# Mask added by TensorE, convolution tiles per pair of channel blocks, and a recurrent unit without reciprocal, in a two-part transformer kernel

## The reference

```python
# recurrent unit of the even layer (width 512, both directions)
log_a = -LRU_C * gate_a * softplus(-lam)
a = exp(log_a)
mult = sqrt(-expm1(2.0 * log_a))
u = mult * gate_x * xc
# h_f, h_b: scans of h = a * h + u forwards and backwards; the result is h_f + h_b

# neighbourhood attention of the odd layer (16 heads of 64, 4 rows of 64 columns)
col_start = clip(cols - NA_WIN_C // 2, 0, GRID_W - NA_WIN_C)
col_mask = (cols[None] >= col_start[:, None]) & (cols[None] < col_start[:, None] + NA_WIN_C)
logits = einsum(q_row, k_blk) * scale + bias
logits = where(col_mask, logits, -inf)
p = softmax(logits)
out = einsum(p, v_blk)

# convolution layer of the second block (512 tokens in two halves)
bgate, cgate, xv = split(h @ w_in, 3)
y = (bgate * dwconv3(cgate * xv, k)) @ w_out
```

## Time and profile before

| | before |
|---|---|
| median of 3 runs | 2204.56 us (2203.05 to 2204.77) |
| profiled execution, its own time | 2202.74 us |
| span of the profiled execution | 2200.9 us |
| busy: PE, DVE, ACT, POOL | 1945.0, 1435.3, 685.0, 149.4 us |
| mean granted clock of PE | 0.933 |

### The profile page before, as it was taken

The page is one execution under the profiler, slowest core; times in us unless marked ns, Lnnn a source line. Parts: engine busy times, 40 slices in busy tenths (PEclk is TensorE's granted clock), DMA queues, the critical chain, the costliest instruction groups (busy, mean ns, idle before and its releaser), DMA issues.

```text
span 2200.9 us, 26847 instructions
## 1 busy us (share of the span) xinstructions
PE 1945.0 (88%) x10068; PEld 1639.4 (74%) x10068; DVE 1435.3 (65%) x2081; ACT 685.0 (31%) x918; POOL 149.4 (7%) x73
## 2 busy tenths in 40 slices
PE   2971787779999998995899999989999998788998
PEld 2951787378888887884688888878888887568998
DVE  7877788787666667448866666676665227455554
ACT  2443343432222223223322222232222223244442
POOL 1000221020000010002200000100000010000000
PEclk9975798679999999998899999999999999799999
DMA  9830685033343443331333334433333224014444
GB/s 378 321 117 0 191 267 200 1 143 126 148 147 139 152 165 135 148 149 69 112 143 145 145 145 163 166 115 143 143 144 127 92 104 164 19 39 141 170 163 157
DMA packets 75731, 315.66 MB, mean 143 GB/s; under 512 B 19060, under 2 KB 22904, under 8 KB 56344
## 3 DMA queue, kind: packets, MB, share of 16 engines
q1 hardware_dynamic: 75136, 314.15, 39.9%
q10 hardware_dynamic: 536, 0.79, 0.1%
HBM read 313.86 MB, written 1.06 MB: 143 GB/s over the span
## 4 chain that ended last, share of the span: by engine, by line
PE 75%; DVE 15%; ACT 4%; issue 3%; DMA 1%; POOL 1%; SPq 0%; DVEq 0%; ACTq 0%
PE acc L1165 71%; DVE Wl L740 3%; PE psN L1165 2%; ACT Wh L501 2%; DVE tmp L727 2%; DVE psGT L772 1%; DVE psGT L769 1%; DVE psGT L775 1%; DMA afirst<-in_ada_w 1%; DVE XT L727 1%; PE psT L1265 1%; DMA raw<-in_odd_in 1%; DVE cy L727 1%; PE psN L1223 1%; DVE gates L1058 1%
## 5 line engine op out<-in xcount | busy, mean ns | idle before, releaser
L1165 PE MATMUL acc<-Hh,Wh 128*128 128x512 f32 (+1 forms) x2400 | 838.5, 349 | 106.8 <-DVE Hl L921 34.8
L1165 PE MATMUL acc<-Hl,Wh 128*128 128x512 f32 (+1 forms) x2400 | 832.5, 347 | 0.0
L1165 PE MATMUL acc<-Hh,Wl 128*128 128x512 f32 (+1 forms) x2400 | 831.9, 347 | 0.0
L740 DVE TENSOR_TENSOR Wl<-raw,Wh 128x2048 fp32r<-128x2048 f32 (+1 forms) x214 | 447.7, 2092 | 296.8 <-ACT Wh L501 296.7
L1165 PEld LDWEIGHTS acc<-Hh,Wh 128*128 128x128 f32 x2400 | 464.6, 194 | 172.5 <-issue 101.1
L1165 PEld LDWEIGHTS acc<-Hl,Wh 128*128 128x128 f32 x2400 | 464.8, 194 | 53.0
L1165 PEld LDWEIGHTS acc<-Hh,Wl 128*128 128x128 f32 x2400 | 464.2, 193 | 53.6
L501 ACT ACTIVATE Wh<-raw 128x2048 fp32r<-128x2048 f32 (+1 forms) x214 | 374.4, 1750 | 360.4 <-PE acc L1165 346.4
L1165 PE MATMUL acc<-hidh,Wh 128*128 128x512 f32 (+1 forms) x704 | 258.6, 367 | 0.9 <-DVE Wl L740 0.9
L1165 PE MATMUL acc<-hidl,Wh 128*128 128x512 f32 (+1 forms) x704 | 258.3, 367 | 0.0
L1165 PE MATMUL acc<-hidh,Wl 128*128 128x512 f32 (+1 forms) x704 | 258.2, 367 | 0.0
(11 more groups left out here) (198 smaller groups left out, 1064.9 us busy)
## 6 DMA issues: line engine op xcount, KB each, us to landing
raw<-in_ffn_up SPq DMA_DIRECT2D x88, 1024.0 KB, 4.7
graw<-in_mod_w SPq DMA_DIRECT2D x144, 512.0 KB, 5.4
raw<-in_ffn_down SPq DMA_DIRECT2D x64, 704.0 KB, 4.1
graw<-in_ada_w SPq DMA_DIRECT2D x32, 512.0 KB, 5.5
raw<-in_odd_in SPq DMA_DIRECT2D x16, 1024.0 KB, 4.9
raw<-in_even_in SPq DMA_DIRECT2D x12, 1024.0 KB, 5.8
raw<-in_conv_in SPq DMA_DIRECT2D x12, 1024.0 KB, 4.7
afirst<-in_ada_w SPq DMA_DIRECT2D x8, 1024.0 KB, 13.1
```

Source lines behind the costliest of these rows:

```text
L740: nc.vector.tensor_tensor(Wl[:, half, 0:f], raw[:, slot, 0:f], Wh[:, half, 0:f].bitcast(f32), ALU.subtract)\
L1165: return nc.tensor.matmul(out, lhsT, rhs, start=start, stop=stop)
```

## The change

Three edits, each in one layer.

1. Neighbourhood attention: POOL makes a small mask `namask` of 128 x 64 once, after `even_out` has read its input. ACT copies it four times side by side, rounded, into `namaskr`, and the identity into `identr`. PE adds it to the scores: before each score matmul of a head there is one of the identity with the mask, into the same bank. `nab` is no longer touched by POOL.
2. Convolution: the tiles of `conv_in` are loaded and multiplied in the order b, c, x for each pair of channel blocks. After each third tile POOL multiplies its pair, ACT scales the centre during the next tile, DVE's taps and ACT's rounding follow one tile later, and DVE's rest another tile later. The results go to buffers of their own (`cyh`, `cyl`), which `conv_out` reads. The stage is written out in full on SP, ACT and DVE.
3. Recurrent unit: `decay(u)` (the exp and the tanh of block u) stands in the attention's unit u on ACT. The multiplier is now (a * a + 1) * tanh in place of a division, and it stands on DVE ahead of the norm's mean.

In the diff the first `beside_conv_in` is ACT's, the second DVE's.

```diff
-            pool.wait_ge(ld_nab, 12 * 16)
-            nb = nab[:, :, :].rearrange("p h (i k) -> p (h i) k", k=HD)
+            pool.wait_ge(h_ready, H0["even_out"] + KC)
+            nc.gpsimd.memset(namask[:, :], 0.0).then_inc(na_bias, 1)
...
+                    part = namask[p, lo:hi]
+                    nc.gpsimd.affine_select(out=part, in_=part, compare_op=ALU.is_ge, fill=MASKED, base=base + step * lo,
+                                            pattern=[[step, hi - lo]], channel_multiplier=ch).then_inc(na_bias, 1)
...
-            pool.wait_ge(drained["act"], S["conv_in"].drained1)
             for k in range(KC):
+                if k % 2 == 0:
+                    pool.wait_ge(drained["act"], S["conv_in"].drained0 + 3 * (k // 2) + 3)
                 nc.gpsimd.tensor_tensor(cv[:, 16 + k, :], cv[:, 8 + k, :], cv[:, 16 + k, :], ALU.mult).then_inc(cv_center, 1)
...
                     exps(a, u + 1)
+                    if beside:
+                        beside(u)
                     copies(a, u)
...
+            def decay(i):
                 nc.scalar.activation(aT[:, i, :], gates[:, 0, i, :], ACT.Exp, scale=lsc[:, 32 + i:33 + i], bias=lsc[:, 32 + i:33 + i])
-                ins = nc.scalar.activation(tT[:, i, :], gates[:, 0, i, :], ACT.Tanh, scale=sp4[:, i:i + 1], bias=sp4[:, i:i + 1])
-            ins.then_inc(lru_at, 1)
+                nc.scalar.activation(tT[:, i, :], gates[:, 0, i, :], ACT.Tanh, scale=sp4[:, i:i + 1], bias=sp4[:, i:i + 1]).then_inc(lru_at, 1)
+            attention(diff, decay)
...
+            act.wait_ge(na_bias, 5)
+            nc.scalar.activation(identr[:, :], ident[:, :], ACT.Copy)
+            for i in range(4):
+                ins = nc.scalar.activation(namaskr[:, i, :], namask[:, :], ACT.Copy)
+            ins.then_inc(na_masked, 1)
...
+            def beside_conv_in(t):
+                if t >= 3 and t % 3 == 0:
+                    for k in range(2 * (t // 3) - 2, 2 * (t // 3)):
+                        conv_center(k)
+                if t >= 4 and t % 3 == 1:
+                    for k in range(2 * (t // 3) - 2, 2 * (t // 3)):
+                        conv_hi(k)
...
+            dve.wait_ge(lru_at, 8)
+            d_ = gates[:, 0, :, :]
+            link(nc.vector.tensor_tensor(d_, aT[:, :, :], aT[:, :, :], ALU.mult))
+            link(stt(tT[:, :, :], d_, 1.0, tT[:, :, :], ALU.add, ALU.mult))
+            nc.vector.tensor_scalar(tT[:, :, :], tT[:, :, :], 1e-30, None, ALU.max).then_inc(lru_m2, 1)
             dve.wait_ge(ot_ss, 1)
             nc.vector.tensor_scalar(means[:, 0:8], psN[:, 0:8], 1.0 / P, EPS, ALU.mult, ALU.add).then_inc(ot_mean, 1)
-            dve.wait_ge(lru_at, 1)
-            d_ = gates[:, 0, :, :]
-            link(nc.vector.tensor_scalar(d_, tT[:, :, :], 1.0, 0.5, ALU.add, ALU.mult))
-            link(nc.vector.reciprocal(d_, d_))
-            link(nc.vector.tensor_tensor(tT[:, :, :], tT[:, :, :], d_, ALU.mult))
-            nc.vector.tensor_scalar(tT[:, :, :], tT[:, :, :], 1e-30, None, ALU.max).then_inc(lru_m2, 1)
...
+            def beside_conv_in(t):
+                if t >= 4 and t % 3 == 1:
+                    for k in range(2 * (t // 3) - 2, 2 * (t // 3)):
+                        conv_taps(k)
+                if t >= 5 and t % 3 == 2:
+                    for k in range(2 * (t // 3) - 2, 2 * (t // 3)):
+                        conv_lo(k)
+            splits(S["conv_in"], beside_conv_in)
+            conv_taps(6)
+            conv_taps(7)
+            conv_lo(6)
+            conv_lo(7)
...
                 for m in range(a.maps):
-                    ins = mm(acc[u % 2][m][:, 0:a.keys], a.q(g, m, qb), a.k(g, m), True, True)
+                    if a is na:
+                        mm(acc[u % 2][m][:, 0:a.keys], identr[:, :], namaskr[:, :, :].rearrange("p i k -> p (i k)"), True, False)
+                    ins = mm(acc[u % 2][m][:, 0:a.keys], a.q(g, m, qb), a.k(g, m), a is not na, True)
...
-            linear(S["conv_out"])
+            linear(S["conv_out"], xh=cyh, xl=cyl)
```

More of the change, by code:

```diff
@@ L294, in summed_of, with conv_tile @@
             return X_TO.get(s.name)
+        def conv_tile(t):
+            return t % 3 * 4 + t // 3
         SPLIT_EARLY = {S[n].n0 + 1 for n in NORMS}
@@ L347, in load @@
                     sp.wait_ge(lo_ready, w)
+                if s.name == "conv_in":
+                    t = conv_tile(t)
                 src = A[s.name][bass.ds(t, 1), :, :].rearrange("a p n -> (a p) n") if not isinstance(t, int) else A[s.name][t, :, :]
@@ L415, in step @@
                             load_bias(*divmod(j, 6))
-                tiles(sp, s, PER, LEAD, step, head={"even_in": 1, "odd_in": 2}.get(s.name, 0))
+                tiles(sp, s, PER, LEAD, step, head={"even_in": 1, "odd_in": 2, "conv_in": 3}.get(s.name, 0))
             sp.wait_ge(drained["dve"], S["ffn3_down"].drained1)
@@ L601, in copies, with attention @@
                 ins.then_inc(a.copied, 1)
-            def attention(a):
+            def attention(a, beside=None):
                 exps(a, 0)
@@ L646, in _ @@
                                      ACT.Tanh, scale=0.5, bias=lsc[:, 16 + i:17 + i]).then_inc(ev_thx, 1)
-            attention(diff)
             act.wait_ge(ev_thx, 16)
-            for i in range(8):
+            def decay(i):
                 nc.scalar.activation(aT[:, i, :], gates[:, 0, i, :], ACT.Exp, scale=lsc[:, 32 + i:33 + i], bias=lsc[:, 32 + i:33 + i])
-                ins = nc.scalar.activation(tT[:, i, :], gates[:, 0, i, :], ACT.Tanh, scale=sp4[:, i:i + 1], bias=sp4[:, i:i + 1])
-            ins.then_inc(lru_at, 1)
+                nc.scalar.activation(tT[:, i, :], gates[:, 0, i, :], ACT.Tanh, scale=sp4[:, i:i + 1], bias=sp4[:, i:i + 1]).then_inc(lru_at, 1)
+            attention(diff, decay)
             act.wait_ge(diff.taken, 4)
@@ L678, in _, with conv_center, conv_hi @@
             norm("conv_in")
-            project(S["conv_in"], lambda m: at(cv, m))
-            for k in range(KC + 1):
-                if k < KC:
-                    act.wait_ge(cv_center, k + 1)
-                    if k >= 2:
-                        act.wait_ge(h_ready, H0["conv_out"] + k - 1)
-                    nc.scalar.activation(cy[:, k % 2, :], cv[:, 16 + k, :], ACT.Copy, scale=V("conv_k", 3 * k + 1)).then_inc(cv_y, 1)
-                if k >= 1:
-                    act.wait_ge(cv_out, k)
-                    nc.scalar.activation(Hh[:, k - 1, :], cy[:, (k - 1) % 2, :], ACT.Copy).then_inc(cv_hi, 1)
+            def conv_center(k):
+                act.wait_ge(cv_center, k + 1)
+                if k >= 2:
+                    act.wait_ge(h_ready, H0["conv_out"] + k - 1)
+                nc.scalar.activation(cy[:, k % 2, :], cv[:, 16 + k, :], ACT.Copy, scale=V("conv_k", 3 * k + 1)).then_inc(cv_y, 1)
+            def conv_hi(k):
+                act.wait_ge(cv_out, k + 1)
+                nc.scalar.activation(cyh[:, k, :], cy[:, k % 2, :], ACT.Copy).then_inc(cv_hi, 1)
+            def beside_conv_in(t):
[5 more added lines that the diff above has]
+                        conv_hi(k)
+            project(S["conv_in"], lambda m: cv[:, 2 * conv_tile(m // 2) + m % 2, :], beside_conv_in)
+            conv_center(6)
+            conv_center(7)
+            conv_hi(6)
+            conv_hi(7)
             splits(S["conv_out"])
@@ L1099, in _, with conv_taps @@
             norm("conv_in", lambda: mod_scale(0, 1))
-            splits(S["conv_in"])
-            dve.wait_ge(drained["act"], S["conv_in"].drained1)
-            def rest(k):
-                dve.wait_ge(cv_hi, k + 1)
-                nc.vector.tensor_tensor(Hl[:, k, :], cy[:, k % 2, :], Hh[:, k, :].bitcast(f32), ALU.subtract).then_inc(h_ready, 1)
-            for k in range(KC):
+            def conv_taps(k):
                 dve.wait_ge(cv_y, k + 1)
@@ L1173, in three, with linear @@
                 return mm(out, wl, xh, False, last)
-            def linear(s, together=False):
+            def linear(s, together=False, xh=Hh, xl=Hl):
                 if together:
@@ L1189, in step @@
                         for j in range(2):
-                            last = three(acc[u % 2][j][:, 0:s.tokens], u % 2, j * KC + k, Hh[:, k, c], Hl[:, k, c], k == 0, k == KC - 1)
+                            last = three(acc[u % 2][j][:, 0:s.tokens], u % 2, j * KC + k, xh[:, k, c], xl[:, k, c], k == 0, k == KC - 1)
                     last.then_inc(tile_done, 1)
@@ L1332, in _ @@
             pe.wait_ge(na.vcopied, 4)
+            pe.wait_ge(na_masked, 1)
             attention(na)
```

27 lines of the change are left out of this document (13 added, 14 removed).

## The result

The changed kernel takes 2169.68 us (median of 4 runs, 2165.03 to 2171.77) against 2203.81 us (4 runs, 2202.37 to 2204.77): ratio 0.9843, 95% interval 0.9825 to 0.9860. It is faster by 34.1 us, where 51.5 was forecast, and 2169.7 lies outside the range of 2143 to 2161. The profiled execution took 2171.77 us with a span of 2169.9 us.

The account below looks back on a forecast made before the run. PE was taken to carry 75% of the chain, so edits pay only where it waits for another engine. Gains 27.9 + 15.3 + 15.8 = 59.0, less 7.5, net 51.5: 2202.74 to 2151.2 us, range 2143 to 2161.

Parts of the forecast that it names:

- the term for the mask matmuls: Neighbourhood attention: masks on PE end the two heads' overlap and give back 7.5 us, bounds 2.8 and 19.2.
- The prediction's own sign of a slower kernel: Stretch between odd_in and odd_out, 65.3 us before, growing by over 14 us would make the kernel slower.
- the rival in which they still do: Neighbourhood attention: heads still overlap, masks cost only their own columns, 2.8 us, total 2146.5 us; chance 0.20.
- the price of a unit: Neighbourhood attention: masks and lost overlap add 1.2 us per unit at half clock to 1.23, half that at full clock.
- Not every unit counts: Neighbourhood attention: scores behind an even unit lie beside DVE's work; six ahead of a mix and two at the start count.
- five at 1.2 and three at 0.5: Neighbourhood attention: eight counted units split by the mean clock of 0.68 between half and full clock, 7.5 us in sum.
- the masks cost all units: Neighbourhood attention: even units' scores outgrow their cover, or mode changes cost as much again; 14 us, total 2158; chance 0.15.
- Convolution: From conv_in's end to the next `Wl`: only the last pair of blocks stays behind, `Wl` 27.9 us earlier, moved work free.
- the rival of a delayed stage: Convolution: moved work makes `Wl` slip 2.5 us in each of three tiles, 7.5 us lost, total 2158.7; chance 0.06.
- Recurrent unit: Even layer, gates' products to DVE's `OT`: norm's result taken up 15.9 us earlier, net 15.3 gained.
- the decays: Attention of the even layer: decays in ACT's units delay copies and mixes by 0.6 us in sum, bounds 0 and 1.4.
- `odd_in`: Without POOL's masks six tiles take 34.9 us in place of 50.7, 15.8 gained.

Follow-up runs that it names:

- experiment 3: Changed kernel with both 128-row masks of a unit ahead of both its scores: 2146.58 us, ratio 0.9740.
- experiment 5: Changed kernel with masks of 64 rows, each in its head's half of the array, order mask, score, mask, score kept: 2142.86 us, ratio 0.9725.
- experiment 12: Kernel before with the recurrent part alone, but the sixteen decays behind the attention on ACT as before: 2189.30 us, ratio 0.9933.
- experiment 1: Changed kernel with the mask matmuls left out, so the neighbourhood attention has no window: 2147.44 us, ratio 0.9743.
- experiment 4: Changed kernel with masks of 64 rows, both ahead of both scores of a unit: 2146.22 us, ratio 0.9737.
- experiment 6: Changed kernel with 64-row masks both ahead of the scores, and the norm's mean moved between DVE's two products: 2142.83 us, ratio 0.9716.
- experiment 8: Kernel before with the convolution part alone: 2179.29 us, ratio 0.9886.
- experiment 10: Changed kernel with 64-row masks, each ahead of its score, and the norm's mean moved between DVE's two products: 2142.62 us, ratio 0.9719.
- experiment 11: Changed kernel with 128-row masks kept in units 0 to 7 and 64-row masks in units 8 to 15, same order: 2155.70 us, ratio 0.9784.
- experiment 2: Changed kernel with the mask written by POOL into the bias during odd_in as before, the two other edits kept: 2162.78 us, ratio 0.9809.
- experiment 7: Kernel before with the mask part alone: 2208.80 us over 10 runs, ratio 1.0015.
- experiment 9: Kernel before with the recurrent part alone (product for reciprocal, decays in the attention's units, mean behind the product): 2188.10 us, ratio 0.9926.

## Why the prediction was wrong

**The step that failed** is the term for the mask matmuls, 7.5 us; it was 21.9 (59.8 to 81.7 in the stretch), above its own upper bound of 19.2. The prediction's own sign of a slower kernel came with it: from the end of `odd_in` to `odd_out` it was 65.3 us and is 87.6 (430.74 - 343.12), 22.3 more, where over 14 was the sign. The mechanism was named rightly, the heads no longer overlap, and the rival in which they still do is refuted by 363.13 - 361.98 = 1.15 us for a lone head. Two sizes in it were wrong.

First, the price of a unit: 1.23 us plus 1.2 was forecast at half clock, 2.43, and 3.30 came. The two masks were put at 0.35 and took 1.00: their average was read from a long row of like matmuls, where loads hide, and even side by side two masks of 128 rows take 0.71. The two scores were put at 2.07, from four rows over the whole array, and took 2.30. The changed kernel's first units show that this isn't the clock alone. Timeline of PE at full clock:

```profile
349.06 0.39 PE L1197 MATMUL acc<-namaskr,identr 128*128 128x256 f32 x1 [0.69 <-ACT natok L686]
...
350.94 0.38 PE L1197 MATMUL acc<-namaskr,identr 128*128 128x256 f32 x1
```

A unit takes 350.94 - 349.06 = 1.88 us there, 1.18 more than its 0.70 before; 0.5 was forecast.

Second, "Not every unit counts". Eight of sixteen were counted, since scores behind an even unit lie beside DVE's work. That asks whether one unit's scores still fit under their cover, and not whether PE's whole round still fits under DVE's. At half clock a pair of units is now two transposes (1.05 and 1.04), two units (3.02 each on the chain) and a mix (1.91): 10.05 us. That is longer than the 7.0 us in which DVE and PE together went round before. So PE became the bound, all sixteen units counted, and the granted clock was 0.50 throughout, with PE busy 62.50 of 65 us. Why it stayed there isn't shown: in `conv_in` PE was busy 133.00 of 134 us at 0.98, so a high busy share alone doesn't bring the lower level. The forecast's "five at 1.2 and three at 0.5" took the clock of before, 0.68, for a stretch whose load the change raised. How the 21.9 us divide between the dearer units and the lower clock isn't settled, since no kernel here had one without the other. An estimate from rows at full clock says that the level mattered: two transposes of 0.67, two units of 1.88 and a mix of 1.12 (at 404.03 in the chain before) are 6.2 us, under the 7.0, so at that level PE's round alone would not have been the bound.

The rival "the masks cost all units" had this mechanism and a place in the range, but a price of 14 us. That the changes themselves cost as much again was in it too; experiment 3 against the changed kernel puts two more of them at 0.29 us per unit, and the lost overlap at 1.15. The Trainium skill, TensorEngine Tiling (Array Packing), section Key Properties, says both that tiles work independently and that a change of tiling mode drains TensorE. These runs agree with both: rows of the two halves side by side in experiments 3 and 5, and loads that stand idle 0.22 to 0.65 us and begin only with their matmul at each change here.

**The other steps held.** Convolution: 10.4 us from drain to `Wl` as forecast, 27.9 gained, with the work inside `conv_in` at no cost (133.1 us); the rival of a delayed stage is out. Contention of POOL with the taps was small: 1.79 us in place of 1.53. Recurrent unit: 29.1 - 13.2 = 15.9 between gates and `OT` as forecast. The gates' products start 1.44 us later than before, but the attention's first scores, ahead of any decay, already start 1.58 later (141.25 and 139.67). The attention takes 30.3 us from there to the gates' products and took 30.5, so the decays cost nothing that shows, where 0.6 was forecast. Alone the part gave 16.3. But the share of the decays' place was overrated when experiment 12 was planned: it has 1.2 where its expectation had 3. `odd_in`: from its first tile to its last it was 111.5 us (262.34 to 373.82) and is 95.4 (247.68 to 343.12), 16.0 for 15.8. POOL's four small masks take 4.84 us where 0.2 was the estimate by size:

```profile
205.40 4.84 POOL L469 TENSOR_SCALAR_AFFINE_SELECT namask<-namask 64x48 f32<-64x48 f32 x4 [0.16 <-POOL namask L462]
```

That is 1.21 each, nearly all fixed cost, and hidden beside the first tile of `even_out` as forecast.

With 21.9 in place of 7.5 the sum is 2202.7 - 59.0 + 21.9 = 2165.6, the fastest of the four runs; the profiled one is 6 us longer. Some 3 of these are in the grouped attention of the last layer. Chain that ended last, changed kernel:

```profile
1922.26 3.69 PE psN L1197 x8
...
1928.85 3.49 PE psN L1197 x8
```

Its last two mixes take 3.69 and 3.49 us where they took 2.01 and 1.99 before. The same is in the traces of experiments 1, 4, 6, 8, 10 and 11, and not in those of 2, 3, 5, 7, 9 and 12. The kernels without the convolution edit (before, 7, 9 and 12) never show it, and seven of the ten with it do, its part alone among them; with one trace of each kernel the cause stays open. These 3 us are as large as the differences between several of the experiments. The rest includes one late load in a layer that the change doesn't touch (5.65 us on the chain, `raw` of `ffn_down`, at 2127.19).

## What to carry to other kernels

A matmul that is added to save work elsewhere should use the rows of the array that its neighbours use: here the same mask in 64 rows cost nothing that could be told, and in 128 rows, between the two heads, it ate 22 of 57 us gained. Before adding work to an engine that waits, add up its whole round, at the lower clock level too, and compare it with the round of the engine that it waits for; a gap at one instruction says nothing about the sum. An edit in three parts should be run in its parts: one of the three was a loss, and the total hid it.

## What was not expected of the hardware

A score of one head over 64 rows takes as long as those of both heads side by side: 1.15 us at half clock. Two masks of 128 rows in a row take 0.71 us at half clock and 0.42 at full clock, two of 64 rows 0.38 at half clock, where they begin together: masks in the two halves overlap as scores do. A change between 128 and 64 rows costs some 0.14 us each at half clock (0.29 for two, with the load that can't go ahead) beyond the lost overlap.

The power on POOL over 128 x 8 numbers took 3.62 us where it started beside a product of DVE over two arrays in the state buffer (SBUF), with 176.49 + 2.28 - 176.65 = 2.1 us of it still to come, in experiments 6 and 10 alike. In the changed kernel a shorter such product (179.96, 1.22 us) lay beside its first 1.06 us, and it took 2.55, as much as before. The Trainium skill, SBUF — State Buffer, section SBUF: two separate sides, says that DVE and GpSimd share a pair of ports as an exclusive lock: whichever starts first holds it for its whole instruction, a DVE instruction with two inputs in SBUF among them. The direction agrees with it. The size does so only in part: POOL took 1.07 more, not 2.1. By an estimate from these rows both cases fit if POOL needs the ports only some 1.05 us after its start (2.12 - 1.07); that isn't seen here.

A GpSimd select over 64 x 48 numbers took 1.21 us and one over 64 x 4608 took 5.87, so 96 times the size costs not quite 5 times the time.
